# A two-layer hybrid decoder on one core: load order of the output stages, key waits by pieces, and tile order in the search

## The reference, cut to what matters

```
proj = h @ w_in;  c_q, c_kv, k_idx = rms_norm(parts of proj);  gate = rest of proj
score[t,s] = sum_h w[t,h] * relu(q_idx[t,h] . k_idx[s])      # 8 heads, causal
sel = top_k(score, 256)                                      # per query
q = c_q @ w_uq;  q_abs = q . w_uk;  p = softmax(q_abs . c_kv[sel] + bias)   # 16 heads
y = ((p . c_kv[sel]) . w_uv * silu(gate)) @ w_out
```

## Time and profile before

| | |
|---|---|
| time, 3 runs | 3884.29 us median, 3883.88 to 3887.35 |
| profiled execution | 3887.83 us, its span 3886.0 us |
| PE busy | 3448.4 us, 89% |
| DVE busy | 2143.9 us, 55% |
| ACT busy | 2016.0 us, 52% |
| POOL busy | 524.2 us, 13% |
| mean granted clock of TensorE | 0.932 of full speed |
| moved by DMA | 436.41 MB, 112 GB/s over the span |

### The profile page before, as it was taken

One profiled execution on the slowest core, in us unless ns is written; L12 is line 12 of the kernel. 1 busy time (PEld: TensorE's weight loads), 2 busy tenths in 40 slices (PEclk: granted clock), 3 DMA queues, 4 the chain that ended last, 5 costly groups with the idle time before them and its releaser, 6 DMA issues. The chain is left out here.

```text
span 3886.0 us, 65323 instructions
## 1 busy us (share of the span) xinstructions
PE 3448.4 (89%) x18786; PEld 2575.8 (66%) x18786; DVE 2143.9 (55%) x5870; ACT 2016.0 (52%) x3490; POOL 524.2 (13%) x550
## 2 busy tenths in 40 slices
PE   6869798878999999996975999999978899889699
PEld 3746454466666666664855888889956666666587
DVE  3659799995555556554644111000077777777344
ACT  2548689965777777774224111111156666666222
POOL 2000255101111111110211111111020000000011
PEclk7989899977999999998987999999989999999799
DMA  8651677663233222324532444322142222220342
GB/s 231 181 135 33 194 224 230 182 211 103 80 83 81 79 75 81 83 76 138 173 135 93 117 122 118 92 70 68 57 127 69 72 69 72 69 69 30 134 140 98
DMA packets 428415, 436.41 MB, mean 112 GB/s; under 512 B 81697, under 2 KB 341185, under 8 KB 427457
## 3 DMA queue, kind: packets, MB, share of 16 engines
q1 hardware_dynamic: 417440, 430.93, 37.4%
q10 hardware_dynamic: 10784, 3.18, 0.8%
HBM read 271.44 MB, written 162.53 MB: 112 GB/s over the span
## 5 line engine op out<-in xcount | busy, mean ns | idle before, releaser
L1253 DVE CUSTOM_DVE_ANT_0 a_att_sb_lg<-a_att_ps_s,mask 128x512 f32<-128x512 f32 (+3 forms) x512 | 302.0, 595 | 220.5 <-PE a_att_ps_s L1144 179.6
L1150 PE MATMUL b_att_ps_s<-b_att_sb_k,b_att_sb_q 64*128 64x512 f32 (+3 forms) x1920 | 295.2, 418 | 84.7 <-DVE b_att_sb_lg L1255 64.0
L1327 ACT ACTIVATE a_att_sb_pT<-a_att_ps_t 128x512 f32<-128x512 f32 (+3 forms) x640 | 316.0, 530 | 104.2 <-PE a_att_ps_t L1163 97.3
L1319 ACT ACTIVATE b_att_sb_lg<-b_att_sb_lg,b_att_sb_negm 128x384 f32<-128x384 f32 (+15 forms) x256 | 305.6, 1198 | 122.6 <-DVE b_att_sb_negm L1261 122.5
L1319 ACT ACTIVATE a_att_sb_lg<-a_att_sb_lg,a_att_sb_negm 128x384 f32<-128x384 f32 (+15 forms) x256 | 307.3, 1200 | 77.5 <-DVE a_att_sb_negm L1261 77.5
L1163 PE MATMUL a_att_ps_t<-ident,a_att_sb_lg 128*128 128x128 f32 x2176 | 339.8, 279 | 0.0
L1255 DVE TENSOR_SCALAR_CACHE_REDUCE b_att_sb_lg<-b_att_ps_s 128x512 f32<-128x512 f32 (+3 forms) x512 | 282.8, 590 | 95.8 <-PE b_att_ps_s L1150 80.4
L1682 DVE TENSOR_SCALAR_CACHE_REDUCE mask<-scores,threshold_bits 128x384 bf16<-128x384 f32 (+8 forms) x288 | 322.5, 1186 | 1.2
L1163 PEld LDWEIGHTS a_att_ps_t<-ident,a_att_sb_lg 128*128 128x128 f32 x2176 | 248.6, 141 | 107.4 <-issue 57.2
L1143 PE MATMUL a_att_ps_s<-a_att_sb_k,a_att_sb_q 128*128 128x512 f32 (+3 forms) x640 | 287.1, 449 | 30.9 <-DVE a_att_sb_mx L1253 16.4
L1180 PE MATMUL a_att_ps_o<-a_att_sb_pT,a_att_sb_v 128*64 128x256 f32 (+1 forms) x2304 | 297.4, 377 | 0.0
(11 more groups left out here) (282 smaller groups left out, 6896.4 us busy)
## 6 DMA issues: line engine op xcount, KB each, us to landing
a_att_sb_q<-scratch_qT SPq DMA_DIRECT2D x512, 64.0 KB, 2.5
select_sb_w_gate<-in_a_w_in SPq DMA_DIRECT2D x32, 512.0 KB, 4.9
mask_sb_mod_w<-in_mod_w SPq DMA_DIRECT2D x16, 1024.0 KB, 6.6
a_att_sb_k<-scratch_kT SPq DMA_DIRECT2D x128, 128.0 KB, 2.8
b_qkgv_sb_w<-in_b_w_in SPq DMA_DIRECT2D x32, 512.0 KB, 4.8
b_att_sb_q<-scratch_qT SPq DMA_DIRECT2D x128, 128.0 KB, 2.5
b_att_sb_k<-scratch_kT SPq DMA_DIRECT2D x64, 256.0 KB, 4.0
front_sb_mod_w<-in_mod_w SPq DMA_DIRECT2D x8, 1024.0 KB, 8.5
```

Source lines behind the costliest of these rows:

```text
L1150: mm = nc.tensor.matmul(s_ps[:, (n + m) % SR, 0:z - a], q[rows, p // 2 % QS, x, cols], k[rows, slot, y, a:z], start=(j == 0), stop=(j == 2))
L1253: x = nc.vector.tensor_tensor_reduce(out, src, tab, 1.0, 2 * NEG, sign, ALU.max, top[:, col:col + 1])
L1319: nc.scalar.activation(buf, buf, ACT.Exp, bias=negm[:, p, m:m + 1], accum_out=sums[:, b, ds(h * M + m, 1)]).then_inc(exp_done, 1)
L1327: nc.scalar.activation(pT[:, r % 2, a:z, c:c + P], t_ps[:, n % TR, 0:z - a], ACT.Copy).then_inc(t_left, 1)
```

## The change

Three edits, in five stages.

1. Search: the gate tile is the last of a pass instead of the first. Tiles of pass s leave PSUM in pass s + 1; those of the last pass leave behind it. The latents are loaded in four pieces by token groups, each with its semaphore, and hidden states and gate weights between them. SP's points for the next gate weights and hidden states move with the gate tile.
2. Attention: one semaphore for each key piece; TensorE waits for piece i at the first block whose logits read it. At the start the key pieces are issued between the q pairs, and the bias table behind piece 0.
3. Output: SP issues values, gates and x of group 0 ahead of the weights, and the gain row behind them, with its own semaphore. ScalarE and VectorE prepare group 0 before they split the weights.

```
+FIRST_READER = [next(p for p in range(NB) if NCH[p] > i) for i in range(KPIECES)]
...
             load_q(0, 0)
-            for piece in range(KPIECES):
-                load_k(0, piece)
+            load_k(0, 0)
             load_near(0)
             for r in range(1, QS):
                 load_q(0, r)
+                load_k(0, r)
...
+                if p == FIRST_READER[i]:
+                    pe.wait_ge(k_in[i], h * 32 + 32)
...
                 if h is not None and p == 0:
-                    pe.wait_ge(k_in, (h + 1) * (32 * KPIECES))
                     logits(h, 0, 0, par)
...
-    TILES = [tile for s in range(PASSES) for tile in [(None, "gate", s % KD, s // KD)] + SMALL_TILES[3 * s:3 * s + 3]]
+    TILES = [tile for s in range(PASSES) for tile in SMALL_TILES[3 * s:3 * s + 3] + [(None, "gate", s % KD, s // KD)]]
...
+            def load_latents(g):
+                cols = slice(g * 512, (g + 1) * 512)
+                for part, buf in ((0, cq_hi), (1, cq_lo)):
+                    sp.dma_start(buf.bitcast(F32)[:, :, cols], cqT[part].rearrange("(k p) t -> p k t", p=P)[:, :, cols]).then_inc(cq_in[g], 16)
+
             load_weights(0)
-            for part, buf in ((0, cq_hi), (1, cq_lo)):
-                sp.dma_start(buf.bitcast(F32)[:], cqT[part].rearrange("(k p) t -> p k t", p=P)).then_inc(cq_in, 16)
+            load_latents(0)
+            load_latents(1)
             load_weights(1)
+            load_latents(2)
             load_gate_weights(0)
             for k in range(KD):
                 load_h(0, k)
+            load_latents(3)
             load_gate_weights(1)
...
-                if t % PER_PASS == 1 and t // PER_PASS + 2 < PASSES:
+                s = t // PER_PASS - 1
+                if t % PER_PASS == 0 and 0 <= s < PASSES - 2:
                     sp.wait_ge(multiplied, t)
-                    load_gate_weights(t // PER_PASS + 2)
-                if t % PER_PASS == 1 and t // PER_PASS % KD == KD - 2 and t // PER_PASS + 2 < PASSES:
+                    load_gate_weights(s + 2)
+                if t % PER_PASS == 0 and s % KD == KD - 2 and 0 <= s < PASSES - 2:
...
+                if x == 0:
+                    pe.wait_ge(cq_in[g], 32)
...
-                    if a >= NA - PER_PASS:
-                        leave(s * PER_PASS + a - (NA - PER_PASS))
+                    if a >= NA - PER_PASS and s:
+                        leave((s - 1) * PER_PASS + a - (NA - PER_PASS))
+            for t in range((PASSES - 1) * PER_PASS, PASSES * PER_PASS):
+                leave(t)
...
-            for k in range(K0, KD // 2):
+            if M == 2:
+                sp.dma_start(gcol[:], subln.rearrange("o p -> p o"), allow_slow_non_contiguous=True).then_inc(gcol_in, 16)
+            load(0, 0, True)
+            for k in range(K0, KD):
                 sp.dma_start(w[:, k - K0], weights[k * P:(k + 1) * P, :]).then_inc(w_in[k], 16)
-            if M == 2:
-                sp.dma_start(gcol[:], subln.rearrange("o p -> p o"), allow_slow_non_contiguous=True).then_inc(consts_in, 16)
-            load(0, 0, True)
-            sp.dma_start(gp[:], gp_row).then_inc(consts_in, 16)
-            for k in range(max(K0, KD // 2), KD):
-                sp.dma_start(w[:, k - K0], weights[k * P:(k + 1) * P, :]).then_inc(w_in[k], 16)
+            sp.dma_start(gp[:], gp_row).then_inc(gp_in, 16)
...
+            after(act, consts_set, M)
+            prepare(0, 0)
             for k in range(K0, KD):
                 after(act, w_in[k], 16)
                 nc.scalar.activation(w_hi[k], w[:, k - K0], ACT.Copy).then_inc(w_hi_done, 1)
-            after(act, consts_set, M)
-            prepare(0, 0)
             groups(act, step)
...
             widen(0)
             prepare(0, 0)
+            for k in range(K0, KD):
+                after(dve, w_hi_done, k - K0 + 1)
+                nc.vector.tensor_tensor(w_lo[k], w[:, k - K0], w_hi[k], ALU.subtract).then_inc(w_lo_done, 1)
+            after(dve, gp_in, 16)
             groups(dve, step)
```

More of the change, by code:

```diff
@@ L963, in stage_attention @@
         s_ps, t_ps, o_ps = st.ps("s", [P, SR, 512]), st.ps("t", [P, TR, 4, P]), st.ps("o", [P, OR, 512])
-        k_in, near_in, near_done, s_done, s_left, dve_chain, max_done, exp_done, mixed, mix_chain, turned, t_left, pv_quad, half_done, o_left, masked, mx_set = (
-            st.sem(n) for n in ("k_in", "near_in", "near_done", "s_done", "s_left", "dve_chain", "max_done", "exp_done", "mixed", "mix_chain",
+        near_in, near_done, s_done, s_left, dve_chain, max_done, exp_done, mixed, mix_chain, turned, t_left, pv_quad, half_done, o_left, masked, mx_set = (
+            st.sem(n) for n in ("near_in", "near_done", "s_done", "s_left", "dve_chain", "max_done", "exp_done", "mixed", "mix_chain",
                                 "turned", "t_left", "pv_quad", "half_done", "o_left", "masked", "mx_set"))
-        q_in, v_in, o_stored = ([st.sem(f"{n}{u}") for u in range(c)] for n, c in (("q_in", QS), ("v_in", 4), ("o_stored", OS)))
+        q_in, k_in, v_in, o_stored = ([st.sem(f"{n}{u}") for u in range(c)] for n, c in (("q_in", QS), ("k_in", KPIECES), ("v_in", 4), ("o_stored", OS)))
         idle_sp, idle_dve, idle_pool = st.sem("idle_sp"), st.sem("idle_dve"), st.sem("idle_pool")
@@ L1022, in load_k @@
                     for part in range(2):
-                        sp.dma_start(dst[part * HD:(part + 1) * HD].bitcast(F32), k_dram[part, ds(h * HD, HD), keys]).then_inc(k_in, 16)
+                        sp.dma_start(dst[part * HD:(part + 1) * HD].bitcast(F32), k_dram[part, ds(h * HD, HD), keys]).then_inc(k_in[piece], 16)
                 else:
@@ L1026, in load_k @@
                         dst = k[:, ds(h % 2, 1), part, keys].rearrange("p o t -> p (o t)")
-                        sp.dma_start(dst.bitcast(F32), k_dram[part, ds(h * P, P), keys]).then_inc(k_in, 16)
+                        sp.dma_start(dst.bitcast(F32), k_dram[part, ds(h * P, P), keys]).then_inc(k_in[piece], 16)
             def load_near(h):
@@ L1501, in stage_select @@
         acc = st.ps("acc", [P, RA, 512])
-        cq_in, ckv_in, w_hi_done, w_lo_done, multiplied, left, hi_done, lo_done, counted_dve, counted_act, chain, tried, h_used = (
-            st.sem(n) for n in ("cq_in", "ckv_in", "w_hi_done", "w_lo_done", "multiplied", "left", "hi_done", "lo_done", "counted_dve", "counted_act",
+        ckv_in, w_hi_done, w_lo_done, multiplied, left, hi_done, lo_done, counted_dve, counted_act, chain, tried, h_used = (
+            st.sem(n) for n in ("ckv_in", "w_hi_done", "w_lo_done", "multiplied", "left", "hi_done", "lo_done", "counted_dve", "counted_act",
                                 "chain", "tried", "h_used"))
-        w_in, h_in, gate_in, stored = ([st.sem(f"{n}{u}") for u in range(c)] for n, c in (("w_in", 2), ("h_in", KD), ("gate_in", 2), ("stored", RO)))
+        w_in, cq_in, h_in, gate_in, stored = ([st.sem(f"{n}{u}") for u in range(c)] for n, c in (("w_in", 2), ("cq_in", G), ("h_in", KD), ("gate_in", 2), ("stored", RO)))
         block = st.block()
@@ L1540, in _ @@
                     load_weights(x + 2)
-                if t % PER_PASS == 1 and t // PER_PASS + 2 < PASSES:
+                s = t // PER_PASS - 1
+                if t % PER_PASS == 0 and 0 <= s < PASSES - 2:
                     sp.wait_ge(multiplied, t)
-                    load_gate_weights(t // PER_PASS + 2)
-                if t % PER_PASS == 1 and t // PER_PASS % KD == KD - 2 and t // PER_PASS + 2 < PASSES:
-                    last, group = t + PER_PASS - 1, t // PER_PASS // KD
+                    load_gate_weights(s + 2)
+                if t % PER_PASS == 0 and s % KD == KD - 2 and 0 <= s < PASSES - 2:
+                    last, group = t + PER_PASS - 1, s // KD
                     for k in range(KD - 1):
@@ L1611, in tile @@
                     pe.wait_ge(w_lo_done, x + 1)
-                    if x == 0:
-                        pe.wait_ge(cq_in, 32)
-                    elif kind == "k" and n == 0:
+                    if kind == "k" and n == 0:
                         pe.wait_ge(ckv_in, 32)
+                if x == 0:
+                    pe.wait_ge(cq_in[g], 32)
                 if t >= RA:
@@ L2158, in step @@
                 norm(g, 1)
-            for k in range(K0, KD):
-                after(dve, w_hi_done, k - K0 + 1)
-                nc.vector.tensor_tensor(w_lo[k], w[:, k - K0], w_hi[k], ALU.subtract).then_inc(w_lo_done, 1)
-            after(dve, consts_in, 16 * M)
             if M == 2:
+                after(dve, gcol_in, 16)
                 nc.vector.tensor_scalar(gcol[:], gcol[:], 1.0 - LAMBDA_INIT, None, ALU.mult).then_inc(gcol_set, 1)
```

4 lines of the change are left out of this document (2 added, 2 removed).

## The result

The changed kernel takes 3832.36 us (median of 5 runs, 3829.8 to 3842.31), the kernel before 3884.29 on the same chip (5 runs, 3881.31 to 3891.74): ratio 0.9869, 95% interval 0.9852 to 0.9886, 51.9 us less. The forecast was 3824, its range 3811 to 3852. The profiled execution took 3832.36 around a span of 3830.6.

What follows compares the result with a forecast made beforehand. TensorE, busy in 89% of the span, bounds mid sparse attention; VectorE sets search passes; stage starts wait for loads. Gains 29.3 (search) + 3.8 + 4.5 + 13 + 10.1 = 60.7 off 3884.3 give 3824 us, range 3811 to 3852.

Steps and rivals of the forecast that it cites:

- Pass 0: Search start: with the gate tile last and tiles leaving a pass later, it holds no eviction; gain 22.2 us.
- The waits for stores: Search: the start of evictions in pass 1 costs 1 us; waits for stores and gate weights keep 3.0 us.
- The chain beside the splits: Search: weight splits push GpSimd's third split into VectorE's 14 column instructions at pass end; 5.5 us stay.
- The passes together: Search, 31 passes: of 20.1 us above 31 x 10.96, 8.5 stay and 11.6 go; ends 0 and 18.
- The mechanism of the splits: Search: a 14 column VectorE instruction takes 1.28 us instead of 0.18 beside GpSimd's split; the gate tile has no split.
- The end: Search: the last four tiles leave after the last pass; cost 3.5 us, ends 2 and 6.
- Gate weights a pass late: Rival, search: weight load, gate tile and q tiles run one after another, 16.8 us a pass; 3980 us, chance 0.05.
- Attentions: Stage starts: sparse attention's bias table and first keys come earlier, gain 3.8 us; differential attention's bias table earlier, gain 4.5.
- the price of the waits: Rival, attentions: TensorE's added waits cost as much as the one gap seen, 27 us; 3851 us, chance 0.08.
- Output stages: First: preparation lies under the weights' transfer, gain 13 us; second: squares as values land, head sums earlier, gain 10.1.
- the search gives little but pass 0: Rival: GpSimd's splits still delay VectorE, or tiles come late; search gains 16 instead of 29; 3837 us, chance 0.18.
- The "more" case: Rival: no split meets VectorE's end-of-pass instructions in the search, differential attention gains 6.5 us; 3812 us, chance 0.08.

## Why the prediction was right, and where it was off

- **Pass 0.** Forecast gain 22.2, measured 32.88 - 10.58 = 22.3.
- **The waits for stores are the term that was mis-sized.** Of the start of the evictions the prediction says "Either that holds or it costs up to 4; I take 1", and it has 3.0 "of waits for stores and gate weights" for the passes: 4.0 in all. From pass 1 on VectorE waits 10.6 us for ScalarE (6.42, 0.80, 2.16 and 1.26 us in passes 2, 9, 17 and 25; 2.9 in all in the kernel before), and each time ScalarE stands for a store. The tile itself came as forecast: 22.2 us after the stage's first load, which is 437.6 on the clock of the kernel before, inside "near 435 to 438", and no wait shows ahead of its eviction. The working looked at the loads' effect on the tiles and never followed the tiles' stores into the same queue, where 9.8 MB of loads stand. Before, the first store was issued at 441.62, when only the last load was still to land (at 443.9), and landed in 3.0. Evictions began 11 us earlier in the stage (14.5 us after its first load instead of 25.6), and their stores met the backlog. Four buffers and the later latents, each by itself, took the slip of pass 2 away.
- **The chain beside the splits.** Forecast: 5.5 us stay. Above 0.17 each, the chain's instructions sum to 6.4 us, 16.9 in the kernel before. But 5.5 was put on weight splits that push the third split into the chain, and 4.0 of the 6.4 stand right behind the late evictions of passes 2, 9 and 17, whose splits come late too; only 2.5 are left behind the other passes, and most passes are 10.96, with q tiles too, where 11.3 was forecast. Behind the reload of the hidden states it looks so (SP's issue, ScalarE's wait for the store, VectorE's wait and the chain beside the late split; then ScalarE behind the two later reloads):
```profile
510.42 6.19 SPq L1527 DMA_DIRECT2D select_sb_h<-scratch_hT  x8
...
528.75 0.60 ACT L1656 ACTIVATE select_sb_o_plain<-select_ps_acc 128x512 f32<-128x512 f32 x1 [0.80 <-DMA scratch_gateT<-select_sb_o_plain]
...
531.43 0.35 DVE L1698 TENSOR_TENSOR threshold_over<-threshold_cnt,threshold_enough 128x14 f32<-128x14 f32 x1 [0.80 <-ACT mask L1664]
...
532.02 1.12 DVE L1711 TENSOR_TENSOR threshold_bits<-threshold_flipped,threshold_picked 128x14 int32<-128x14 int32 x1
...
620.09 0.60 ACT L1656 ACTIVATE select_sb_o_plain<-select_ps_acc 128x512 f32<-128x512 f32 x1 [2.15 <-DMA scratch_gateT<-select_sb_o_plain]
...
702.30 0.60 ACT L1656 ACTIVATE select_sb_o_plain<-select_ps_acc 128x512 f32<-128x512 f32 x1 [1.75 <-DMA scratch_v<-select_sb_o_plain]
```
- **The passes together.** They take 356.67, 16.9 above 31 x 10.96, where the forecast had 9.5. That 8.6 are left when passes 2 and 3 (17.34 + 12.88, 8.3 above two of 10.96) are taken out, next to the forecast's 8.5, is chance: 6.8 of them are passes 9, 10, 17, 18 and 25, behind the reloads.
- **The mechanism of the splits** was read rightly: no 14 column instruction is above 0.6 in a pass without such a slip, and putting the gate tile first again brings 10.9 us of it back. The Trainium skill's rule (SBUF — State Buffer, "Who interferes with whom") agrees: the counts, 611 to 1811 ns as before, keep their length beside splits, and the 14 column instructions do not. By the rule alone a split beside counts costs nothing; what is left where evictions were in time is the 2.5.
- **The end.** Forecast cost 3.5. The last chain starts at 778.73 and the mask stage at 785.76, 7.03 against 2.85: 4.2, with the wait for the gate store named. The search's sum is then 22.3 + (20.1 - 16.9) - 4.2 = 21.3 in this pair of profiles, against 29.3:
```profile
781.50 1.09 ACT L1656 ACTIVATE select_sb_o_plain<-select_ps_acc 128x512 f32<-128x512 f32 x2 [1.55 <-DMA scratch_gateT<-select_sb_o_plain]
```
- **Gate weights a pass late,** the rival on the slower side: TensorE waits for gate weights in many passes, up to 3.15 us, but no eviction of the changed kernel waits for TensorE. The cover held. The rival's 3980 was summed wrongly: 161 is measured against the present passes, so the 11.6 may not be taken off again, and 3992 comes out.
- **Attentions.** 3.8 and 4.5 against 3.7 and 5.3. First product 4.13 us earlier (10.88 to 6.75), stage 3.7 shorter by the means, 3.1 by this pair: no more than 0.4 to 1.1 can be the price of the waits, where the rival had 27. That rival set the upper bound of the range. In differential attention VectorE starts 5.55 earlier, 1 more than the bytes removed gave; where this 1 comes from is open.
- **Output stages.** 13 and 10.1 against 12.9 and 9.5. In the second the head sums came 9.3 earlier instead of 10.1; the late weight splits went into TensorE's wait before the next head sums, which is 1.38 us now (2.45 before).
- **The rival "the search gives little but pass 0"** (3837) came nearer to the truth for a reason that it did not name. With its 16 the sum misses by 4 on the one side, with 29 by 9 on the other. The "more" case (3812) does not add up: its named parts, 18 instead of 11.6 and 6.5 instead of 4.5, are 8.4 and not 12, which makes 3816.

## What to carry to other kernels

When evictions move forward, follow their stores: here the first gate store, issued while loads were still on their way, landed 10.9 us after its issue instead of 3.0, and ScalarE stood for the buffer that it frees. Give each kind of tile a buffer of its own, so that a wait goes one round back and not to the tile ahead; here 2 KB a partition were worth 11 us. And move the engines' order together with that of the loads: the loads alone gave 1 us of 13 in one output stage and nothing that shows in the other.

## What was not expected of the hardware

- An issue on SP mostly took 0.45 us in the search, and 5.17 for a 1 MB load with 3.4 MB ahead of it (7.6 issued, 4.2 moved; 425.36 above). It is not the size of the load: with the latents loaded later, a load of 128 KB took 4.92 us to issue at the same place. SP itself then stands, and every store behind it. The view of that kernel:
```profile
428.63 4.92 SPq L1520 DMA_DIRECT2D select_sb_w<-in_a_w_uq  x1
```
- 0.5 MB pieces with rows of 2 KB moved 286 GB/s where 2 MB loads with rows of 8 KB moved 338 in the same ten us, although all were queued one behind another.
- The same code in a stage where TensorE binds varies by 5.5 us from kernel to kernel (777.5 to 783.0 in differential attention), the search by 1.8. In the second output stage a group of tokens takes 27.7 us in some places and 30.9 in others, in one execution. A part worth under 6 us is told from its own stage's start, not from the whole.
